# Splitting next-stage weight pieces early and spreading the modulation column sums in a two-layer encoder kernel

## The reference

```python
def reference(x, c, mod_w, mod_b, norm_g, ...):
    for i in range(DEPTH):
        mod = jax.nn.silu(c) @ mod_w[i] + mod_b[i]
        sh_m, sc_m, g_m, sh_f, sc_f, g_f = [m[:, None, :] for m in jnp.split(mod, 6, axis=-1)]
        h = rms_norm(x, norm_g[i, 0]) * (1 + sc_m) + sh_m
        ...
            y = fox_attention(h, fox_w_in[j], fox_b_f[j], fox_w_out[j])      # layer 0
        ...
            y = rwkv7_time_mix(h, rwkv_mu[j], ...)                           # layer 1
        x = x + g_m * rms_norm(y, norm_g[i, 1])
        h = rms_norm(x, norm_g[i, 2]) * (1 + sc_f) + sh_f
        y = conv_ffn(h, ffn_w_in[i], ffn_conv_w[i], ffn_conv_b[i], ffn_w_out[i])
        x = x + g_f * rms_norm(y, norm_g[i, 3])
    return x

def conv_ffn(h, w_in, conv_w, conv_b, w_out):
    u = h @ w_in
    ...
    x1, x2 = jnp.split(u, 2, axis=-1)
    return (jax.nn.gelu(x1, approximate=False) * x2) @ w_out
```

## Time and profile before

| | |
|---|---|
| time, median of 3 runs | 2973.27 us (2972.95 to 2982.41) |
| the profiled execution, its own time | 2986.54 us |
| its span in the trace | 2984.7 us |
| PE busy | 2786.3 us, 93% of the span |
| DVE, ACT, POOL busy | 70%, 48%, 5% |
| TensorE clock granted, mean | 0.959 of full speed |
| DMA, mean over the span | 213 GB/s |

### The profile page before, as it was taken

One profiled execution on the slowest core, in us unless ns is written; L12 is line 12 of the kernel. 1 busy time (PEld: TensorE's weight loads), 2 busy tenths in 40 slices (PEclk: granted clock), 3 DMA queues, 4 the chain that ended last, 5 costly groups with the idle time before them and its releaser, 6 DMA issues.

```text
span 2984.7 us, 57070 instructions
## 1 busy us (share of the span) xinstructions
PE 2786.3 (93%) x22010; PEld 2454.6 (82%) x22010; DVE 2089.3 (70%) x2726; ACT 1426.2 (48%) x1977; POOL 144.1 (5%) x160
## 2 busy tenths in 40 slices
PE   4599999899999999996999999997989999999998
PEld 3499997688888888885988788886878888888887
DVE  7877787888888766567864454554887666666565
ACT  2143334455555544446754333332456666664433
POOL 0000000000000000000000133130100000000000
PEclk8699999999999999998999999998999999999999
DMA  9968898778888758782555332222956666657785
GB/s 313 320 231 288 283 306 276 264 249 283 277 279 284 220 184 263 232 267 82 188 183 176 123 96 66 89 86 86 346 163 186 186 183 188 185 182 223 242 254 170
DMA packets 513063, 634.28 MB, mean 213 GB/s; under 512 B 27160, under 2 KB 451976, under 8 KB 512648
## 3 DMA queue, kind: packets, MB, share of 16 engines
q1 hardware_dynamic: 508864, 628.94, 64.7%
q10 hardware_dynamic: 4040, 3.07, 0.3%
HBM read 629.83 MB, written 2.10 MB: 212 GB/s over the span
## 4 chain that ended last, share of the span: by engine, by line
PE 76%; DVE 4%; ACT 1%; issue 1%; DMA 0%; SPq 0%; DVEq 0%; ACTq 0%
PE ps L1997 41%; PE ps L2000 21%; PE ps L2179 10%; PE ps L2024 1%; PE ps L2233 1%; PE ps L2015 1%; DVE wlo L1269 0%; DVE mx L1681 0%; PE ps L1981 0%; PE ps L2160 0%; DVE ut L1881 0%; DVE y L1398 0%; DVE rs L1389 0%; DVE x L1404 0%; PE ps L2044 0%
## 5 line engine op out<-in xcount | busy, mean ns | idle before, releaser
L1269 DVE TENSOR_TENSOR wlo<-raw,whi 128x1024 fp32r<-128x1024 f32 x792 | 964.9, 1224 | 500.7 <-ACT whi L816 499.3
L816 ACT ACTIVATE whi<-raw 128x1024 fp32r<-128x1024 f32 x792 | 833.3, 1058 | 888.4 <-PE ps L2000 528.4
L1997 PE MATMUL ps<-xs,whi 128*128 128x512 f32 x3328 | 1175.0, 398 | 29.1 <-DVE xs L1688 15.0
L2000 PE MATMUL ps<-xs,wlo 128*128 128x256 f32 x3328 | 934.1, 281 | 0.0
L1997 PEld LDWEIGHTS ps<-xs,whi 128*128 128x128 f32 x3328 | 627.6, 189 | 182.1 <-issue 27.0
L1997 PE MATMUL ps<-act,whi 128*128 128x512 f32 x1920 | 687.3, 401 | 22.5 <-DVE wlo L1269 22.4
L2000 PEld LDWEIGHTS ps<-xs,wlo 128*128 128x128 f32 x3328 | 631.0, 190 | 0.0
L2000 PE MATMUL ps<-act,wlo 128*128 128x256 f32 x1920 | 544.6, 284 | 0.0
L1997 PEld LDWEIGHTS ps<-act,whi 128*128 128x128 f32 x1920 | 367.0, 191 | 110.8 <-DVE wlo L1269 25.2
L2000 PEld LDWEIGHTS ps<-act,wlo 128*128 128x128 f32 x1920 | 370.0, 193 | 0.0
L1291 DVE SCALAR_TENSOR_TENSOR macc<-raw,cact,macc 128x1024 f32<-128x1024 f32 (+1 forms) x266 | 324.8, 1221 | 12.8 <-DMA raw<-in_mod_w 6.8
(11 more groups left out here) (269 smaller groups left out, 3018.9 us busy)
## 6 DMA issues: line engine op xcount, KB each, us to landing
raw<-in_ffn_w_in SPq DMA_DIRECT2D x352, 512.0 KB, 4.5
raw<-in_mod_w SPq DMA_DIRECT2D x272, 384.0 KB, 4.6
raw<-in_mod_w SPq DMA_DIRECT2D x192, 512.0 KB, 5.9
raw<-in_ffn_w_out SPq DMA_DIRECT2D x176, 512.0 KB, 4.7
raw<-in_fox_w_in SPq DMA_DIRECT2D x96, 512.0 KB, 5.9
raw<-in_fox_w_out SPq DMA_DIRECT2D x32, 512.0 KB, 6.8
raw<-in_rwkv_w_r SPq DMA_DIRECT2D x32, 512.0 KB, 4.2
raw<-in_rwkv_w_k SPq DMA_DIRECT2D x32, 512.0 KB, 3.4
```

Source lines behind the costliest of these rows:

```text
L816: sc.activation(whi[:, half, :, :].rearrange("p k n -> p (k n)"), slots[slot], ACT.Copy).then_inc(w_hi, 1)
L1269: v.tensor_tensor(wlo[:, half, :, :].rearrange("p k n -> p (k n)"), slots[slot], whi[:, half, :, :].rearrange("p k n -> p (k n)").bitcast( ...
L1997: pe.matmul(ps[bank + m][:, :], whi[:, half, k, m * P:m * P + P], src[:, kt, :, :].rearrange("p u s -> p (u s)"), start=kt == 0, stop=Fals ...
L2000: last = pe.matmul(ps[bank + m][:, 0:S], wlo[:, half, k, m * P:m * P + P], src[:, kt, 0, :], start=False, stop=kt == n * PIECE_KT - 1, ski ...
```

## The change

No arithmetic is added or taken away. In the order of the program:

- At the end of the attention stage, of both up projections, of the r and of the k projection, and of three of the four output and down projections (the last has no stage behind it), pieces 0, 1 and 2 of the next stage are split on ACT and DVE while PE still works on the last slab (in the attention stage: ahead of the last softmax), and piece 3 afterwards. Before, pieces 0 to 3 were split behind or between the last steps of the stage; k and v had no early pieces.
- In the output and down projections, the first lap's unit is summed by PE in four parts of two columns, one behind each of the first four pieces of the second lap, and DVE writes `mod` in that lap's second slab. The second lap's unit is summed after the sum of squares, and DVE writes it behind the reciprocal (in the last stage: between `both_halves` and the gate, ahead of the reciprocal).
- ACT's wait for the gate column (`gain`) moves from the head of these stages to its first use.

```diff
-    ph_rkv = [None] + [Phase(4, "W" * 8) for _ in range(2)]
+    ph_rkv = [None] + [Phase(4, "W" * 8, early=3) for _ in range(2)]
```

ACT, in `out_proj` and at the end of the up projection:

```diff
                     if n < 3:
+                        if slab == 0:
+                            sc.wait_ge(*o["v"].at("gain"))
...
-                if n < 3:
-                    sc.wait_ge(*o["v"].at("gain"))
...
+                early(following, 0, 1, 2)
                 sc.activation(rtab[:, :], eps[0], ACT.Sqrt)
                 low_half(NSLAB - 1)
...
-                early(following, 0, 1, 2, 3)
+                early(following, 3)
...
                 gelu(UP_ITERS - 1)
+                early(ph_down[n], 1, 2)
                 side(UP_ITERS - 1, 1)
                 taps(UP_ITERS - 1, 1, s["a2"])
-                early(ph_down[n], 1, 2)
+                early(ph_down[n], 3)
                 product_hi(UP_ITERS - 1)
-                early(ph_down[n], 3)
```

DVE, in `residual`, in `out_proj`, at the end of the up projection, and at the end of r (k, and ACT, alike):

```diff
                 v.wait_ge(*o["v"].at("rinv"))
+                if n < 3:
+                    adaln_out(ph, 1, 0)
...
-                early(following, 0, 1, 2, 3)
+                early(following, 3)
...
+                def first_unit():
+
+                    both_halves(4)
+                    adaln_out(ph, 0, 0)
...
-                    if ph.units:
-                        adaln_out(ph, i, ph.units - 1)
...
+                    if i:
+                        hooks[per_slab + NH - 1] = first_unit
+                    pieces(ph, i, hooks)
+                early(following, 0, 1, 2)
                 both_halves(NSLAB - 1)
                 if n == 3:
+                    adaln_out(ph, 1, 0)
                     gains(n)
...
                 conv(UP_ITERS - 1, 0, s["a1"], s["v1"])
+                early(ph_down[n], 0, 1, 2)
                 joined(UP_ITERS - 1, 1)
-                early(ph_down[n], 0)
                 second_half(UP_ITERS - 1)
-                early(ph_down[n], 1)
+                early(ph_down[n], 3)
                 product_lo(UP_ITERS - 1)
-                early(ph_down[n], 2, 3)
...
+            early(ph_rkv[1], 0, 1, 2)
             result(0, 3, 1)
```

PE, in `out_proj`:

```diff
-                    if ph.units:
-                        adaln_sum(ph, i, ph.units - 1)
+                                    between=(lambda q: adaln_sum(ph, 0, 0, q, 4) if q < 4 else None)
+                                    if i == 1 and s == 0 else None)
...
                 last.then_inc(*o["pe"].inc("sum"))
+                adaln_sum(ph, 1, 0)
```

More of the change, by code:

```diff
@@ L1127, in rkv_body @@
                     for w in range(8):
-                        hi(ph_rkv[j], i, w)
+                        hi_new(ph_rkv[j], i, w)
                         if w == 1 and j == 1:
@@ L1144, in _ @@
                 laps(4, rkv_body)
+                if j == 1:
+                    early(ph_rkv[2], 0, 1, 2)
                 side(j, 3, 1, ph_rkv[j].weight(3, 7))
@@ L1381, in gains, with residual @@
                     *outp[n]["v"].inc("gain"))
-            def residual(n, following):
+            def residual(n, ph, following):
                 o = outp[n]
@@ L1575, in _ @@
                 fox_body(i, False)
+            early(ph_fox_out, 0, 1, 2)
             softmax_max(7)
-            early(ph_fox_out, 0)
             softmax_den(7)
+            probs_out(7)
+            early(ph_fox_out, 3)
+            attn_lo(7)
             adaln_out(ph_fox, 6)
[L1580 to L1584, removed]
             def out_proj(n, ph, following=None):
@@ L1984, in slab, with paired_slab @@
                     last.then_inc(w_used, 1)
-            def paired_slab(ph, i, w0_, bank, src, ready=None, n=4, only=None):
+            def paired_slab(ph, i, w0_, bank, src, ready=None, n=4, only=None, between=None):
                 for q in range(n) if only is None else only:
@@ L2002, in paired_slab, with adaln_sum @@
                     last.then_inc(w_used, 1)
-            def adaln_sum(ph, i, u=0):
-                if ph is ph_chunk:
-                    pe.wait_ge(gemv_out, i + 1)
-                else:
-                    pe.wait_ge(raw_done, ph.done(i, ph.m_at[u * KT + KT - 1]))
-                if not at_start(i, ph.unit0 + u):
-                    pe.wait_ge(mod_written, ph.unit(i, u - 1))
-                n = unit_cols[ph] // P
+                    if between:
+                        between(q)
+            def adaln_sum(ph, i, u=0, part=0, parts=1):
+                n = unit_cols[ph] // P
+                if part == 0:
+                    if ph is ph_chunk:
+                        pe.wait_ge(gemv_out, i + 1)
+                    else:
+                        pe.wait_ge(raw_done, ph.done(i, ph.m_at[u * KT + KT - 1]))
+                    if not at_start(i, ph.unit0 + u):
+                        pe.wait_ge(mod_written, ph.unit(i, u - 1))
                 full = sums(ph)[1]
-                for t in range(n):
+                for t in range(n * part // parts, n * (part + 1) // parts):
                     last = pe.matmul(pmod[:, t:t + 1], full[:, t * P:t * P + P], ones[:, 0:1], start=True, stop=True,
                                      skip_group_check=True)
-                last.then_inc(mod_summed, 1)
+                if part == parts - 1:
+                    last.then_inc(mod_summed, 1)
             def x_sum(n):
```

13 lines of the change are left out of this document (6 added, 7 removed).

## The result

The changed kernel takes 2953.53 us, median of 5 runs (2951.12 to 2960.84), beside 2977.62 for the kernel before on the same chip (5 runs, 2972.95 to 2989.13): ratio 0.9909, 95% interval 0.9884 to 0.9934. That is 24 us by the medians and 27 by the ratio. Forecast were 35.8 us, 2938; the time lies inside the range of 2927 to 2957. The profiled execution fell from a span of 2984.7 us to 2954.0, by 30.7.

The account below looks back on a forecast made before the run. PE's own work plus its losses at borders was taken as the bound. Borders -14.1, laps -4.8, clock -14.2, gate wait and smaller rests -1.5, chains -1.2 sum to -35.8: 2973.3 becomes 2938 us, range 2927 to 2957.

Parts of the forecast that it names:

- Borders without a chain: Up to down, r to k, k to v, attention to its projection: PE goes on at once with pieces split beforehand, -14.1 us.
- lap borders: Four lap borders: PE's rest of 1.39 us goes each time, less 0.8 for cutting the column sums, -4.8 us.
- the splitting: Column sums cut into four at each lap border: extra entry cost of 0.2 us a lap, bounds 0 and 0.4.
- The clock: Seven windows of low granted clock behind PE's rests: they go with the rests, -14.2 us, bounds 0 and -14.2.
- clock stays low: Rival: the border rests go, but low clock has another cause or was rarer in timed runs; 2952 us, chance 0.17.
- Gate wait: Entry of the time mixing's output projection: ACT's idle 0.84 us for the gate column goes, -0.9 us with the handover.
- The four chains: Reduction chains ending the output and down projections: changed work ahead of `y` or the last reciprocal, -1.2 us in all.
- wrong if ACT waits for a transfer in an early `hi`: Sign against the prediction: the last slab's copy, DVE and PE would all stand behind that wait; no size given.
- The table load of 1.28 us, no drain: ACT's table load in the chains: 1.28 us as traced; at the skill's 2.66 us, 2.4 us less gain.
- Feed binds: Rival: DMA limits the two wide projections once PE no longer pauses, some 7 us come back; 2945 us, chance 0.11.
- From profile to timed runs: Whole kernel: the saving of 35.8 us from the profiled execution was applied unchanged to the timed median of 2973.3.

Follow-up runs that it names:

- The halves measured alone: Kernel before with only the early pieces at borders without a reduction chain: ratio 0.9930; with only the first lap's column sums in four parts: 0.9955.
- the filled kernel: Kernel before with unused matmuls on constants filling PE's rests at the borders, nothing else: 2977.87 us against 2978.49, ratio 0.9994.
- Undoing the ends: Changed kernel with the next stage's early pieces split behind the residual in the attention's and time mixing's output projections: 2934.39 us, repeated 2940.33.

## Why the prediction came out as it did

- **Borders without a chain, -14.1, and lap borders, -4.8: right.** The rests are gone to the last one. The column sums stand as four rows of 4 records and 0.50 us each in the second lap of the attention's projection (at 517.74, 520.97, 524.19 and 527.41), 2.0 us against 1.84 in one piece, so the 0.2 for the splitting holds. The halves measured alone gave 21 and 13 us with their clock. From the first weight matmul to the last slab, attention, layer 0, time mixing (r to its output projection) and layer 1 took 8.3, 9.7, 12.1 and 6.1 us less, 36.2; my terms for them add up to 34.6. Part of the first is chance: the same stretch took between 492 and 505 us in the profiles of the changed kernel and its variants.
- **The clock, -14.2: mechanism right, size 12.9.** The windows go with the rests, as the filled kernel shows too. I took half of each window's length; at 640 against 347 to 353 ns a pair it is 45%. In the profile the term came in: the rests (20.4 with the splitting and the gate wait, as I sized them) and 12.9 make 33.3 of the 36.2. In timed runs it is not shown by itself: the filled kernel gained nothing measurable (0.9976 to 1.0011), with 1.5 us of new waits and 6.5 of slow rhythm against it. The rival "clock stays low" was near in time (2952), and by luck: the windows that I counted did go.
- **Gate wait, -0.9: right.** ACT's `hi` follows at 2057.66 without a wait, PE's rest there fell from 6.8 to 5.9.
- **The four chains, -1.2: the step that failed.** Up to `x_sum` they cost +2.7: +2.5 at the attention's end (I took -1.2), -2.0 in the down projection (-1.0), +1.8 at the time mixing's end (+0.6), +0.4 in the last stage (+0.4, on the number). For the attention's end I gave the two bounds +1.3 and -1.6 and chose near the second, since DVE's stops were gone. They did not come back: DVE ended its last `mfin` only 0.3 us earlier against the slab. ACT's three `hi` and table load, which I counted in the down projection, I did not count there, nor the wait for a transfer; `y` came 1.5 later. And the low clock behind PE's rest, for which I had no term, added about 1 at each of the two wide ends through the column sums. The condition "wrong if ACT waits for a transfer in an early `hi`" was written down, but carried no price. Undoing the ends gave 7.7 us at these places. From `x_sum` to the next stage's first weight matmul another 1.5 is lost in the three ends that have one, so the chains cost 4.2; with a start that came 1.3 later, 36.2 - 4.2 - 1.3 is the profiled saving of 30.7.
- **The table load of 1.28 us, no drain: right.** In the down projection it took 1.28 again, with the next operation 0.01 behind it. The Trainium skill, "ScalarE: Activation LUTs", "What ACT_TABLE_LOAD costs", gives about 2.66 us for a switch, drain included; the trace agrees with its part for the load, and the drain does not appear in this case.
- **Feed binds: no.** No rest for `wlo` at any lap border. The feed's transfers were late only in the early `hi` at the two wide ends, where ACT waited 0.49 and 0.39 us.
- **From profile to timed runs: mis-sized.** The profiled saving was 30.7. The profiled execution of before lay 9 us above the median of its runs, that of after 2. Runs of the changed kernel spread from 2937 to 2961, and two profiles of one kernel differ by 12 us through the rhythm of one stage alone; I moved one execution's saving to the median as if neither moved.

## What to carry to other kernels

Work pulled ahead of a critical finishing step must fit on every engine that the step uses, its transfers included: count each engine's load there, and where one is full, put the work behind the step. Rests of the matrix engine at borders are worth removing for their own length. Price the low clock behind them by the start-to-start time of the work's own matmuls at both clocks, and ask what a faster stretch will then wait for. And where two kernels differ in a stage that neither edit touches, compare the start-to-start time of equal matmuls before believing in any cause.

## What was not expected of the hardware

- Back-to-back pairs of 512- and 256-column matmuls ran at 346.7 or 353.3 ns, for as long as 630 us, at full clock and without a gap, and differently in two executions of one kernel. It changes at disturbances alone. A few one-column matmuls without a rest beside them took the slow rhythm away: groups of 4 records (0.50 us) in 18 places of 18, groups of 12 in 9 of 9; the other way it went 3 times of 158 and once of 77. Why stays open.
- 12 one-column matmuls in a row (24 records, 2.73 us) brought the granted clock to 1.2 GHz without any rest, in three places of three. Groups of 12 records (1.3 us) did not.
- In the low windows a pair took 640 ns, in the same work at 2.4 GHz 347 to 353: half the clock is not half the speed here.
